# Moving the new retention state of the last head pair from the mixing branch to the opening of the feed-forward

## The reference, cut to what matters

```python
def _layer(x, pos, s_wkv, s_ret, s_shift, p):
    z = _rmsnorm(x, norm_mix_pre) @ w_in
    ya, s_wkv, s_shift = rwkv7_branch(...)          # branch A
    yb, s_ret = retention_branch(...)               # branch B
    m = sigmoid(ga) * (ya @ w_out_a) + sigmoid(gb) * (yb @ w_out_b)
    x = x + _rmsnorm(m @ w_o, norm_mix_post)        # output product
    h = _rmsnorm(x, norm_ffn_pre)
    f = (silu(h @ w_gate) * (h @ w_up)) @ w_down    # feed-forward
    return x + _rmsnorm(f, norm_ffn_post), s_wkv, s_ret, s_shift

# retention, per head (8 heads, key 64, value 128), g = 1 - 2**(-5-h):
#   o = (q k^T * decay) v + (q S) * decay_q
#   S = S * g**C + (k * decay_k)^T v      the new state: an output of the kernel
```

## Time and profile before

| what | value |
|---|---|
| median of 3 runs | 1286.19 us |
| the profiled execution | 1286.61 us, its span 1284.4 us |
| TensorE, VectorE, ScalarE busy | 95%, 67%, 43% of the span |
| chain that ended last | PE 82%, DVE 10%, ACT 4%, issue 3%, DMA 1% |
| mean granted clock of TensorE | 0.988 of full speed |
| a weight tile | 512 KB, 3.5 us from issue to landing (median) |

### The profile page before, as it was taken

How to read it: one execution, slowest core, us unless ns; L and a number is a source line. 1 busy time by engine, 2 the same in 40 slices (tenths; PEclk the granted TensorE clock), 3 DMA queues, 4 the chain that set the end, 5 groups by cost and what they waited for, 6 DMA issues and landing times.

```text
span 1284.4 us, 27898 instructions
## 1 busy us (share of the span) xinstructions
PE 1223.7 (95%) x12056; PEld 1159.6 (90%) x12056; DVE 859.4 (67%) x1476; ACT 558.1 (43%) x849; POOL 141.3 (11%) x160
## 2 busy tenths in 40 slices
PE   6999899999998999999999998999999989999996
PEld 5999787998998999999898987889889989999996
DVE  4887558888776666653388954688878566666433
ACT  4553345444435433344454544355453453333432
POOL 0004463100000000000000071900100000000000
PEclk9999999999998999999999999999999989999998
DMA  6433134644453545444434424264354435444441
GB/s 212 143 117 117 53 120 152 228 135 145 139 165 115 185 140 159 148 147 150 147 98 131 123 80 110 87 224 148 131 173 126 155 97 164 148 148 149 148 149 71
DMA packets 51177, 179.12 MB, mean 139 GB/s; under 512 B 6256, under 2 KB 7024, under 8 KB 49776
## 3 DMA queue, kind: packets, MB, share of 16 engines
q1 hardware_dynamic: 42576, 153.77, 38.1%
q10 hardware_dynamic: 8480, 23.58, 5.3%
HBM read 166.18 MB, written 8.53 MB: 136 GB/s over the span
## 4 chain that ended last, share of the span: by engine, by line
PE 82%; DVE 10%; ACT 4%; issue 3%; DMA 1%; ACTq 0%; SPq 0%; DVEq 0%
PE dense L1362 51%; PE core L1362 31%; DVE w_lo L890 3%; ACT w_hi L591 2%; DVE x L939 1%; DVE y_out L937 1%; DMA ret_s<-ret_t 1%; DVE ret_t L1288 1%; ACT L579 0%; DMA x<-x_t 0%; DVE bonus L1008 0%; DVE tmp L994 0%; ACT sq_pair L811 0%; DVE bonus L1004 0%; DVE s_ga L1160 0%
## 5 line engine op out<-in xcount | busy, mean ns | idle before, releaser
L890 DVE TENSOR_TENSOR w_lo<-w_raw,w_hi 128x1024 fp32r<-128x1024 f32 x282 | 352.8, 1253 | 222.0 <-ACT w_hi L591 220.8
L591 ACT ACTIVATE w_hi<-w_raw 128x1024 fp32r<-128x1024 f32 x282 | 297.8, 1057 | 446.6 <-PE dense L1362 300.0
L1362 PE MATMUL dense<-h_hi,w_hi 128*128 128x320 f32 x1296 | 416.8, 322 | 22.9 <-DVE h_lo L894 11.4
L1362 PE MATMUL dense<-h_lo,w_hi 128*128 128x320 f32 x1296 | 404.1, 312 | 0.0
L1362 PE MATMUL dense<-h_hi,w_lo 128*128 128x320 f32 x1296 | 404.0, 312 | 0.0
L1362 PEld LDWEIGHTS dense<-h_hi,w_hi 128*128 128x128 f32 x1296 | 246.9, 190 | 43.0 <-issue 35.0
L1362 PEld LDWEIGHTS dense<-h_lo,w_hi 128*128 128x128 f32 x1296 | 247.1, 191 | 1.4 <-issue 0.2
L1362 PEld LDWEIGHTS dense<-h_hi,w_lo 128*128 128x128 f32 x1296 | 246.7, 190 | 0.0
L1362 PE MATMUL core<-h_hi,w_hi 128*128 128x320 f32 x416 | 129.3, 311 | 0.0
L1362 PE MATMUL core<-h_hi,w_lo 128*128 128x320 f32 x416 | 128.9, 310 | 0.0
L1362 PE MATMUL core<-h_lo,w_hi 128*128 128x320 f32 x416 | 128.9, 310 | 0.0
(11 more groups left out here) (299 smaller groups left out, 1982.6 us busy)
## 6 DMA issues: line engine op xcount, KB each, us to landing
w_raw<-wts SPq DMA_DIRECT2D x282, 512.0 KB, 3.5
ret_t<-ret_t ACTq DMA_DIRECT2D x16, 256.0 KB, 3.7
ret_s<-ret_t ACTq DMA_DIRECT2D x16, 256.0 KB, 2.4
ret_rest<-ret_d ACTq DMA_DIRECT2D x2, 1536.0 KB, 8.6
qk_rot<-qk_raw SPq DMA_DIRECT2D x8, 320.0 KB, 6.2
dmask<-rconst ACTq DMA_DIRECT2D x2, 1152.0 KB, 5.6
s_st<-wkv_st ACTq DMA_DIRECT2D x2, 1024.0 KB, 5.0
wkv_s<-s_st ACTq DMA_DIRECT2D x2, 1024.0 KB, 4.2
```

Source lines behind the costliest of these rows:

```text
L591: act.activation(w_hi[n % RING][:, :], w_raw[n % RING][:, :], ACT.Copy).then_inc(hi_ready.sem, 1)
L890: dve.tensor_tensor(w_lo[r][:, :], w_raw[r][:, :], w_hi[r][:, :].bitcast(F32), ALU.subtract).then_inc(low_made.sem, 1)
L1362: return pe.matmul(out, lhsT, rhs, start=start, stop=stop)
```

## The change

For the last pair (`hp` = 3) the state's matmuls move from the mixing branch to the place behind `norm_sum(1)`; the copy and the four products of VectorE move behind low half 5 of gate/up; the three stores move behind the second SiLU of the feed-forward. For pairs 0 to 2 everything stays. `kdk`, `kexp` and the last `retp` get places of their own, `sq8` of the two norms in question gets one too, so that nothing overwrites the state's inputs or `ret_tb` in between. TensorE no longer waits for the update before `variances(3)`, and waits for it when it opens the second group of gate/up. The last pair's parts lie in three banks instead of five; the fourth product waits for the first, with which it shares a bank.

```diff
-        retp = at("retp", 36, 512)
+        retp = [at("retp", 36, 384), at("retp_last", 123.5, 128)]
-        kdk, kexp = at("kdk", 90, 256), at("kexp", 91, 256)
+        kdk, kexp = at("kdk", 124, 256), at("kexp", 125, 256)
-        y_out, sq8 = at("y_out", 85, 8 * T), at("sq8", 95, 8 * T)
+        y_out, sq8, sq8_mixed = at("y_out", 85, 8 * T), at("sq8", 95, 8 * T), at("sq8_mixed", 109, 8 * T)
...
 # ScalarE
+                def store_states(hp):
+                    act.wait_ge(*ret_upd_evac(layer, 2 * hp + 2))
+                    for par in range(2):
+                        act.dma_start(ret_s[layer, 2 * hp + par], ret_tb[par][:, :]).then_inc(rets_stored[par].sem, 16)
...
-                    act.wait_ge(*ret_upd_evac(layer, 2 * hp + 2))
-                    for par in range(2):
-                        act.dma_start(ret_s[layer, 2 * hp + par], ret_tb[par][:, :]).then_inc(rets_stored[par].sem, 16)
+                    if hp + 1 < HP:
+                        store_states(hp)
-                act.dma_start(ret_p[layer], retp[:, :]).then_inc(retp_stored.sem, 16)
+                act.dma_start(ret_p[layer][:, 0:384], retp[0][:, :]).then_inc(retp_stored.sem, 16)
                 roots_b(HP - 1)
...
-                for s in (shift_stored, wkvs_stored, wkvp_stored, retp_stored, *rets_stored):
+                for s in (shift_stored, wkvs_stored, wkvp_stored, retp_stored):
                     act.wait_ge(*s(layer, s.per_layer))
...
+                    if c == 1:
+                        store_states(HP - 1)
+                        act.dma_start(ret_p[layer][:, 384:512], retp[1][:, :]).then_inc(last_stored.sem, 16)
                     if c == 1 and layer + 1 < DEPTH:
                         load_consts(layer + 1)
                 tables(LN_EXP)
+                for s in (last_stored, *rets_stored):
+                    act.wait_ge(*s(layer, s.per_layer))
...
 # VectorE
+                def add_state(hp, to, whole, parts):
+                    dve.wait_ge(*ret_upd(layer, hp + 1))
+                    link(dve.tensor_copy(to, whole))
+                    for par in range(2):
+                        dve.wait_ge(*rett_loaded[par](layer, hp + 1))
+                        for q, of in enumerate((slice(0, 256), slice(256, 512))):
+                            ins = dve.scalar_tensor_tensor(ret_tb[par][:, of], ret_tb[par][:, of], GAMMA8[2 * hp + par],
+                                                           parts[2 * par + q][:, 0:256], ALU.mult, ALU.add)
+                            if q == 0:
+                                link(ins)
+                        ins.then_inc(ret_upd_evac.sem, 1)
+                        dve.wait_ge(*ret_upd_evac(layer, 2 * hp + par + 1))
...
+                    if hp + 1 < HP:
+                        add_state(hp, retp[0][:, 128 * hp:128 * (hp + 1)], core[2][:, 0:128], [core[0], core[3], core[1], core[4]])
                     gate(nxt + 4)
...
                 for n in range(RING, EARLY):
                     low(layer, T_GU + n)
+                add_state(HP - 1, retp[1][:, :], core[3][:, 256:384], [core[2], core[3], core[4], core[2][:, 256:512]])
                 dve.wait_ge(*x_rooted(layer, 2))
...
 # TensorE
                     elif g >= G_GU:
                         pe.wait_ge(*evacuated_by(layer, G_GU - 1))
+                        if g >= G_GU + 4:
+                            pe.wait_ge(*ret_upd_evac(layer, 2 * HP))
...
+                def new_state(hp, whole, parts, ordered=False):
+                    for b in range(2):
+                        for par in range(2):
+                            mm(whole[C * par:C * par + C, :], kdk[:, b * 128 + par * C:b * 128 + (par + 1) * C],
+                               v_block(2 * hp + par, b), b == 0, b == 1)
+                    for n in ((0, 2, 1, 3) if not ordered else range(4)):
+                        par, q = n // 2, n % 2
+                        own = slice(C * par + 32 * q, C * par + 32 * q + 32)
+                        if ordered and n == 3:
+                            pe.wait_ge(*state_begun(layer, 1))
+                        ins = mm(parts[n][:, 0:256], v_sample(hp)[own], kexp[own, :])
+                        if ordered and n == 0:
+                            ins.then_inc(state_begun.sem, 1)
+                    ins.then_inc(ret_upd.sem, 1)
...
                     pe.wait_ge(*mixed_evac(layer, hp + 1))
+                    if hp + 1 < HP:
+                        new_state(hp, core[2][:, 0:128], [core[0], core[3], core[1], core[4]])
                     nxt = fill(FILL[2], nxt)
                 assert nxt == T_WOA
-                pe.wait_ge(*ret_upd_evac(layer, 2 * HP))
                 variances(HP - 1)
...
                 norm_sum(1)
+                new_state(HP - 1, core[3][:, 256:384], [core[2], core[3], core[4], core[2][:, 256:512]], True)
```

More of the change, by code:

```diff
@@ L283, in program @@
         (lora_loaded, shift_loaded, mask_loaded, trig_loaded, s0st_loaded, ret0_first, ret0_rest,
-         shift_stored, wkvs_stored, wkvp_stored, retp_stored) = many(
+         shift_stored, wkvs_stored, wkvp_stored, retp_stored, last_stored) = many(
             1, "lora_loaded", "shift_loaded", "mask_loaded", "trig_loaded", "s0st_loaded",
-            "ret0_first", "ret0_rest", "shift_stored", "wkvs_stored", "wkvp_stored", "retp_stored", unit=16)
+            "ret0_first", "ret0_rest", "shift_stored", "wkvs_stored", "wkvp_stored", "retp_stored", "last_stored", unit=16)
         rcs_loaded, dmask_loaded = many(1, "rcs_loaded", "dmask_loaded", unit=16)
@@ L302, in program @@
         ret_upd_evac, = many(2 * HP, "ret_upd_evac")
+        state_begun, = many(1, "state_begun")
         lora_done, lora_evac = many(12, "lora_done", "lora_evac")
@@ L597, in open_x @@
                     act.activation(ch(h_hi, c), ch(x, c), ACT.Copy, scale=vec_of(layer)(gain, c)).then_inc(h_high.sem, 1)
-                    act.activation(ch(sq8, c), ch(x, c), ACT.Square).then_inc(x_squared.sem, 1)
+                    act.activation(ch(sq8_mixed if k == 2 else sq8, c), ch(x, c), ACT.Square).then_inc(x_squared.sem, 1)
             act.wait_ge(vec_loaded, 16)
@@ L848, in project_out @@
                         act.wait_ge(*finished(layer, g))
-                        act.activation(ch(sq8, c), bank(g)[:, 0:T], ACT.Square).then_inc(y_squared.sem, 1)
+                        act.activation(ch(sq8_mixed if k == 1 else sq8, c), bank(g)[:, 0:T], ACT.Square).then_inc(y_squared.sem, 1)
                         act.activation(ch(y_out, c), bank(g)[:, 0:T], ACT.Copy, scale=vec(gain, c)).then_inc(dense_evac_a.sem, 1)
@@ L880, in _ @@
                     open_x(layer + 1, 1, "mix_pre", lambda c: act.wait_ge(*x_done(layer, X_GROUP_OF[c] + 1)))
-            for s in (shift_stored, wkvs_stored, wkvp_stored, retp_stored, *rets_stored):
+            for s in (shift_stored, wkvs_stored, wkvp_stored, retp_stored, last_stored, *rets_stored):
                 act.wait_ge(s.sem, DEPTH * s.per_layer * 16)
@@ L920, in norm_add @@
                 def norm_add(k, added, lows, after=None):
+                    s8 = sq8_mixed if k == 1 else sq8
                     for c in range(KT):
@@ L924, in norm_add @@
                         if 0 < c < KT - 1:
-                            ins = dve.tensor_tensor(acc[:, :], ch(sq8, 0) if c == 1 else acc[:, :], ch(sq8, c), ALU.add)
+                            ins = dve.tensor_tensor(acc[:, :], ch(s8, 0) if c == 1 else acc[:, :], ch(s8, c), ALU.add)
                             if c < KT - 2:
@@ L1406, in norm_sum @@
                     pe.wait_ge(*y_squared(layer, k * KT))
-                    mm(core[0][:, 0:T], ones, ch(sq8, KT - 1), False, True).then_inc(sum_done.sem, 1)
+                    mm(core[0][:, 0:T], ones, ch(sq8_mixed if k == 1 else sq8, KT - 1), False, True).then_inc(sum_done.sem, 1)
                 def x_sum(k, half):
@@ L1413, in x_sum @@
                         c = 4 * half + j
-                        ins = mm(core[0][32 * j:32 * j + 32, 0:T], ones[:, 0:32], ch(sq8, c), half == 0, half == 1)
+                        ins = mm(core[0][32 * j:32 * j + 32, 0:T], ones[:, 0:32], ch(sq8_mixed if k == 2 else sq8, c), half == 0, half == 1)
                     if half:
```

## The result

The changed kernel takes 1277.48 us (median of 12 runs, 1274.73 to 1281.65) against 1283.92 for the kernel before (12 runs in all, 1280.66 to 1289.71): a ratio of 0.9949, with a 95% interval of 0.9937 to 0.9962, or 6.5 us (4.9 to 8.1). Part of that is the level: three runs gave the kernel before 1286.19, twelve give 2.3 us less. The rest is gain: 6.5 us where 4.9 were forecast.

The account below looks back on a forecast made before the run. The prediction took TensorE, busy for 95% of the span, as the bound. Its terms, 4.2 + 1.1 - 0.4 = 4.9 us, came off 1286.2 to give 1281.3 us, with an 8-in-10 range of 1278.7 to 1283.3.

Parts of the forecast that it names:

- step 3: Feed-forward opening, behind the output product's wait: less work runs at the lower clock, gain 1.1 us, ends 0 and 3.8.
- Step 1: End of pair 3, mixing branch: without the state's matmuls the variances start 2.1 us earlier per layer, 4.2 us in all.
- Rival 3: Projection of branch A: TensorE's wait for `s_ga` grows and gives back the mixing branch's gain; 1285.0 us, chance 0.06.
- Step 2: Wait of 3.72 us behind the output product: the state's matmuls, 1.23 us, go in front of it at cost 0.
- the first rival: Both feed-forward openings: the clock stays up and gives 3.8 us; 1279.0 us in all, chance 0.13.
- the second rival: Both feed-forward openings: the clock falls as before and gives nothing; 1282.4 us in all, chance 0.28.
- Step 4: Second group of gate/up tiles: TensorE's new wait for VectorE's products, 0 to 0.2 us per layer, taken as 0.
- Rival 4: Second group of gate/up tiles: VectorE's late products hold up TensorE in both layers; slower, up to 1293 us, chance 0.03.
- Step 5: ScalarE's queue behind the second SiLU: three store issues delay `w_hi` of tile 6, costing 0.4 us once, in layer 0.

## Why the prediction was wrong

The direction was right and the mechanisms of the steps are seen in the profiles; two sizes were off. The gain was 6.5 instead of 4.9 us, above all by step 3, and the sum started from a level, the median of three runs, that lies 2.3 us above that of twelve. Together that is 3.8 us, and the time fell out of the range. By the gain alone it would not have: 1286.2 - 6.5 = 1279.7 lies inside it.

*Step 1* (4.2): 2.3 us per layer in pair 3 and 0.1 in the projection, 4.8 in all by the stages. The variances came 2.2 us earlier instead of 2.09: the forecast let the fill tile start at 317.58, where the first state matmul stood, but that one started 0.24 us behind the matmul before it, and matmuls of one tile follow each other after 0.147. The fill tile starts 0.10 us earlier than assumed. The variances themselves are another 0.10 shorter (0.84 us to tile 55 instead of 0.94). The wait for `s_ga` went from 0.66 and 0.61 to 0.52 in both layers. Rival 3 is out.

```profile
317.34 0.31 PE L1362 MATMUL dense<-h_hi,w_lo 128*128 128x320 f32 x1
317.58 0.66 PE L1362 MATMUL core<-v_tok,kdk 128*64 128x128 f32 x8
```

*Step 2* (0): right; the matmuls lie in the wait. They take 2.0 us there, not 1.23, which no one waits for.

*Step 3* (1.1) is the step that failed, by its size. Openings of kernels with the kernel before's wait took 23.36, 23.61, 23.30 and 22.65 us, mean 23.2; those with the state's matmuls in the wait and nothing else 21.57, 21.58, 22.41, 21.58, 22.64 and 22.51, mean 22.05. That is 1.2 us per layer, **2.4 in all**. Each mean rests on four or six openings that spread by 1 us, so the 2.4 is an estimate, good to about 1 us. Leaving the matmuls out gave 2.35 us back in the medians, but its two openings (22.65 and 22.54) account for 1.1 of that. The ends of the term (0 and 3.8) held, and 1.85 had been worked out against the profile; it was then cut to 1.1 on the guess that the profile lay near the slow end of the executions. By its time it did lie there (1286.61 us against the median of 1283.92), by the clock hardly (31 us at the lower level by the measure of the table, against 29 in the mean of 39 runs), but what the change does to the clock was guessed from one fall elsewhere. The clock was up in half of the openings with 1.76 us of wait left, where the forecast, on 2.4 us, had expected a fall in most.

The Trainium skill's rule (gaps of over about 3 us, "TensorE: Matmul & The Clock Gate", section "Why this matters for your kernels"), the first rival, does not hold as a bound: waits of 1.76, 1.80 and 2.56 us were followed by falls in some executions. Its 3.8 us for step 3 lie 1.4 above the 2.4 measured, the second rival's 0 lies 2.4 below.

*Step 4* (0, a tie): right to 0.15 us. The products end at 413.62, and TensorE starts the second group at 413.77, 0.35 us behind the pick; it was 0.29 before. Rival 4 is out.

*Step 5* (-0.4): -0.8, shown by the later stores. The slip of `w_hi` of tile 6 was priced at 1.37 us, the length of the three issues in pair 3. It started 4.14 us behind the pick before (423.20 - 419.06) and 5.91 in the changed kernel: 1.77. The three added issues take 1.55 us from the first start (416.21) to the start of the next (417.76), with a gap of 0.32 between the first two, and the three loads behind them 0.16 us more than before. The 0.4 us more went straight onto TensorE, since the slack was used up.

Sum with the measured terms: 4.8 + 2.4 - 0.8 = 6.4 us, against 6.5 (4.9 to 8.1) measured; that they meet within 0.1 is luck, given how loosely the 2.4 is known. The change between the scores of pairs 0 and 2 of layer 1 (50.1 and 50.3 us before, 49.6 and 49.7 changed) would add 0.5; it lies within the interval, and its cause was not sought.

## What to carry to other kernels

Price a wait of TensorE by the work that runs behind it at the lower clock as well as by its length: here two waits of 3.7 us cost another 1.6 us each in the matmuls behind them, and matmuls put into the wait, useful or idle, won that back in part or whole. The wait at the end of layer 0 was no such place: 6.8 us at half clock cost 0 to 0.4 us there, so measure the stage behind a wait at both levels before filling it. Before moving DMA issues, look at what stands behind them on their engine's queue; three issues in front of the next weight tile's rounding took back 0.8 us, and four SiLUs later they are free. Where executions of one kernel spread as widely as the gain, compare stages between landmarks of two profiles and take the level from more than three runs.

## What the runs showed of the hardware

- The same wait leads to different clocks in different executions: with 1.76 us left, the opening ran at full clock three times (1.00 in the rows above) and with a stretch at half three times; with 2.56 us once each way; with 3.10 us it fell in both seen and with 3.7 us in all four, for 3.4 to 6.8 us; with the wait closed to about 0.2 us or less it fell in none of six. One wait alone does not decide it: before the scores of pair 2 of layer 1 a wait of 1.80 us was followed by a fall in the first profile of the kernel before, and one of 1.96 us by none in the second, and in the first profile of the changed kernel the clock was at half in 182 to 184 with no wait over 0.73 us in the 12 us before. Over the runs of each kernel, 1 us more at the lower level goes with 0.3 to 0.45 us more time in most kernels (0.1 in two of them), below the 0.5 that half speed would cost if TensorE bounded all of it.
- A transfer wait that no edit touches. In pair 2 of layer 1 TensorE waits for the state update of pair 1, and in front of it ScalarE waits for the landing of pair 0's `ret_s` store before it loads the next `ret_t` and makes the roots. That pair's two stores took 4.1 us (median) to land in the first profile of the kernel before, 3.6 in the changed, 4.6 with the stores later, and 2.3 with 24 idle matmuls; TensorE's wait was 1.80, 1.31, 3.20 and 0.60 us. In all four kernels with idle matmuls it was 0.6, in the profiles of the kernel before and of the changed one (twice each) 1.3 to 2.0. That explains about 1.3 of the 2.6 us that the openings leave open in the kernel with 24 idle matmuls. The rest of the 2.6, and why the store lands sooner there, stay open: neither was tried.

ScalarE in the kernel before and in the one with 24 idle matmuls:

```profile
885.30 1.28 ACT L579 ACT_TABLE_LOAD   x1 [3.21 <-DMA ret_s<-ret_t]
```
```profile
880.82 1.28 ACT L579 ACT_TABLE_LOAD   x1 [1.42 <-DMA ret_s<-ret_t]
```
